# A three-part transformer program on one core: new SBUF addresses for its stages, with the weights and inner activations of the long stage shifted by 32, 64 and 192 bytes

## The chip, the cores and the metric

One core of one Trainium2 chip. The metric is the device time of one execution in microseconds (us). The profile is one profiled execution of the same program.

## The reference, cut to what matters

Two transformer blocks follow each other on 1024 tokens of width 1024, in fp32. In outline (the three stages that the text names are marked):

```
z = rms_norm(x) @ w_in                      # "pp": projections of block 1, latent queries/keys/values
o_g = gated_linear_attention(...) * silu(g_r)
o_m = latent_attention(...)
h = x + concat(o_g, o_m) @ w_out            # "rm", the long stage, begins here
h = h + square(relu(rms_norm(h) @ w_mlp_up)) @ w_mlp_down
h = h + (p @ w_ple_proj) * sigmoid(rms_norm(h) @ w_ple_gate + b)
q, k, v, z = modulated(rms_norm(h)), modulated(ctx) @ da_w_in      # "rm" ends here
o = softmax differences over 1280 keys, 8 heads                     # "da"
out = rms_norm(h + gate * ((norm(o) * silu(z)) @ da_w_out))         # "hp"
```

## The kernel before, in words

The program is a chain of blocks, each ended by a barrier of all engines: pp (`project_and_prepare`), gla, ma, rm (`residual_to_differential`), da (`differential_attention`), hp (`head_norm_project`). Every fp32 product is made of three fp32r matmuls on a high and a low part: stationary hi with moving hi, stationary hi with moving lo, stationary lo with moving hi (`product`, line 242; lines 874 to 876 in pp). Each matmul comes with its own weight load of 128 columns (PEld); the load for the next matmul runs while the present one streams. Names in the profile read out<-moving,stationary.

**The long stage, rm.** Weight chunks of 128x512 go through a ring `rm_stage` of four (SP loads them, ACT makes `rm_w_hi`, POOL `rm_w_lo`). In order: the output projection (16 tiles of 24 matmuls, x stationary, w moving); eight groups of the MLP, each 8 "up" tiles (24 matmuls each, w stationary, x moving, 512 columns) and then 16 "down" tiles (12 matmuls each, the inner activations `rm_h_hi`/`rm_h_lo` stationary, w moving); the gate (16 tiles of 24, x stationary) and `p @ w_ple_proj` (16 tiles of 6); the projections of block 2: z, q and k (48 tiles of 24, w stationary, x moving), their context tiles (8 tiles of 24 with 256 columns, `ctx_hi`/`ctx_lo` moving), and v (20 tiles of 24, w moving, x stationary in 16 of them, ctx in 4).

**Addresses.** Tensors are given addresses in the order of the `sb(...)` calls, upward and without gaps; what opens in an inner context is placed over what a closed one held. Bytes in a partition, from the declared shapes:

| tensor | before | modulo 512 |
|---|---|---|
| x halves (`xa`, `xb`, hi and lo), all stages | from 50336 | 160 |
| `rm_stage` | 115872 | 160 |
| `rm_w_hi`, `rm_w_lo` | 124064, 156832 | 160, 160 |
| `rm_h_hi`, `rm_h_lo` | 196032, 212416 | 448, 448 |
| `ctx_hi`, `ctx_lo` | 196032, 204224 | 448, 448 |
| `rm_pT`, `rm_proj` | from 196032 | 448 |
| `pp_w_hi`, `pp_w_lo` | 124064, 140448 | 160, 160 |
| da: q, k, v, aT, prob | from 50848 | 160 |
| `hp_w`, x in hp | from 124576, 50848 | 160 |

In every matmul operand a 128-column slice or a row of k is a multiple of 512 bytes, so the remainder above is that of each access. "Distance" below is the stationary operand's address minus the moving one's, modulo 512.

**The end of pp.** For the last token tile (t = 7) PE turns four groups of queries and keys (`turn`, line 916, four transposes each into the one bank `turn_bank`), ACT copies each to `pp_qk_hi` (`high`, line 614), DVE subtracts into `pp_qk_lo` (`low`, line 784), and SP stores both (lines 449, 451). Each `turn` waits until the `low` before it has read the bank. The groups of output columns of pp are taken in the order of `first_col`: two of features, two of `gv`, two of `gr` (the gate, with Silu instead of Copy in `take`, line 573).

Of the kernel before, what the change touches and what calls it, by code (L numbers as in the profile page):

```python
# [12 lines left out]
P = 128  # L13
# [33 lines left out]
class Chip:  # L47
# [7 lines left out]

    def sb(self, name, shape, dt=F32, ctx=None):
        return (ctx or self.ctx).enter_context(self.nc.sbuf_tensor(name, shape, dt))

# [19 lines left out]
    def place_differential(self):  # L78

        keys = S + CTX
        with ExitStack() as ctx:
            sb = lambda name, shape, dt=F32: self.sb("da_" + name, shape, dt, ctx)
            sb("sums_place", [P, DH * TT, 2])
            prob, aT_lo = sb("prob", [P, 4, 2, keys]), sb("aT_lo", [P, 2, keys // P, 2 * P], F32R)
            low_score, inv, ratio = sb("low_score", [P, DH * TT, 2]), sb("inv", [P, DH * TT]), sb("ratio", [P, DH * TT])
            lam_in, lam_prod = sb("lam_in", [P, 2, 2, DD]), sb("lam_prod", [P, 2, DD])
            sb("space_a", [P, 256])
            q0 = sb("q0", [P, 2, S], F32R)  # L90
            k_hi0, v_hi0 = sb("k_hi0", [P, 2, keys], F32R), sb("v_hi0", [P, keys // P, P], F32R)
            sb("space_b", [P, 256])
            q1, v_hi1 = sb("q1", [P, 2, S], F32R), sb("v_hi1", [P, keys // P, P], F32R)
            sb("space_c", [P, 768])
            k_lo0, v_lo0 = sb("k_lo0", [P, 2, keys], F32R), sb("v_lo0", [P, keys // P, P], F32R)
            k_hi1, k_lo1 = sb("k_hi1", [P, 2, keys], F32R), sb("k_lo1", [P, 2, keys], F32R)
            v_lo1 = sb("v_lo1", [P, keys // P, P], F32R)
            aT_hi = sb("aT_hi", [P, 2, keys // P, 2 * P], F32R)
            o_sb = sb("o_sb", [P, 2, NCOL])
        self.da = dict(prob=prob, aT_lo=aT_lo, aT_hi=aT_hi, low_score=low_score, inv=inv, ratio=ratio, lam_in=lam_in,  # L100
                       lam_prod=lam_prod, o_sb=o_sb, q=(q0, q1), k_hi=(k_hi0, k_hi1), k_lo=(k_lo0, k_lo1),
                       v_hi=(v_hi0, v_hi1), v_lo=(v_lo0, v_lo1))
# [39 lines left out]
def constants(nc, chip, a):  # L142

    c = chip
    c.H = c.sb("residual", [P, TT, D])
    c.sums = c.sb("sums", [P, TT])
# [102 lines left out]
def project_and_prepare(nc, chip, a, d):  # L249
# [14 lines left out]
    c_q = g_r + GH * GDV  # L264
    first_col = [None, 0, GW, NCOL, NCOL + GW, g_r, g_r + GW]
    FEATURE = (1, 2)
# [16 lines left out]
    with ExitStack() as ctx:  # L283
# [8 lines left out]
        junk = free[:, at:at + 1280]  # L292
        stage = sb("stage", [P, SLOTS, NCOL])
        piece_stage = stage[:].rearrange("p a (b n) -> p (a b) n", b=2)
        w_hi, w_lo = sb("w_hi", [P, KT, 2 * GW], F32R), sb("w_lo", [P, KT, 2 * GW], F32R)
        with ExitStack() as early:
# [25 lines left out]
        ssh, msh, rsh = sb("ssh", [P, 2, 2, MH]), sb("msh", [P, 2, 2, MH]), sb("rsh", [P, 2, 2, MH])  # L322
        v_hi, v_lo = sb("v_hi", [P, MH, MV], F32R), sb("v_lo", [P, MH, MV], F32R)
        up_bank = c.banks("pp_up", ctx, 4)
        c_bank, turn_bank = c.banks("pp_turn", ctx, 2)
# [27 lines left out]

        tok_of = lambda t: slice(t * P, (t + 1) * P)

        def x_bank(t, b):
# [26 lines left out]
        def result(n):  # L383

            g, o = outs[n]
            bank = p_bank[n % 2]
            if g in FEATURE:
                f, h = divmod(o, HALVES)
                return bank[:], ring[:, n % RING, :], d["gqk"][2 * (g - 1) + f, :, h * NCOL:(h + 1) * NCOL]
            name = "gv" if g < 5 else "gr"  # L390
            cols = slice((g - 3) % 2 * GW, (g - 3) % 2 * GW + GW)
            return bank[:, 0:GW], ring[:, n % RING, 0:GW], d[name][o][:, cols]
# [148 lines left out]
        def _(act):  # L541
# [16 lines left out]
            def take(n):  # L558
# [12 lines left out]
                if n - first_out[1] >= RING:  # L571
                    act.wait_ge(stored[n % RING], 16 * stores_at(n - RING))
                nc.scalar.activation(held, bank, ACT.Silu if g >= 5 else ACT.Copy,
                                     scale=GDK ** -0.5 if g == 1 else 1.0).then_inc(copied, 1)
# [34 lines left out]
            def high(t, m):  # L609
                q, g = divmod(m, 2)  # L610
                act.wait_ge(turned, 4 * t + m + 1)
                if t:
                    act.wait_ge(q_out, 64 * t)
                nc.scalar.activation(qk_hi[:, q, 4 * g:4 * g + 4, :],
                                     turn_bank[0:MQK].rearrange("p (h n) -> p h n", h=4), ACT.Copy).then_inc(hi_ready, 1)

# [61 lines left out]
        def _(dve):  # L678
# [102 lines left out]
            def low(t, m):  # L781
                q, g = divmod(m, 2)
                dve.wait_ge(hi_ready, 4 * t + m + 1)
                nc.vector.tensor_tensor(qk_lo[:, q, 4 * g:4 * g + 4, :],
                                        turn_bank[0:MQK].rearrange("p (h n) -> p h n", h=4),
                                        qk_hi[:, q, 4 * g:4 * g + 4, :].bitcast(F32), ALU.subtract).then_inc(lo_ready, 1)
# [65 lines left out]
        def _(pe):  # L852
# [58 lines left out]
            def turn(t, m):  # L911
                q, g = divmod(m, 2)
                pe.wait_ge(roped, 4 * t + 2 * (q + 1))
                pe.wait_ge(*((lo_ready, 4 * t + m) if 4 * t + m else (x_lo_ready, 2 * TT)))
                for h in range(4):
                    last = nc.tensor.transpose(turn_bank[0:MQK, h * P:(h + 1) * P], nrm[:, t % 2, q, 4 * g + h, :],
                                               c.ident[:])
# [885 lines left out]
def residual_to_differential(nc, chip, a, d):  # L1803
# [58 lines left out]
    with ExitStack() as ctx:  # L1862
        sb = lambda n, s, dt=F32: c.sb("rm_" + n, s, dt, ctx=ctx)
        sem = lambda n: c.sem("rm_" + n, ctx)
        stage = sb("stage", [P, SLOTS, NCOL])
        w_hi, w_lo = sb("w_hi", [P, 2, KT, NCOL], F32R), sb("w_lo", [P, 2, KT, NCOL], F32R)
        act_r = sb("act_r", [P, 2, NCOL])
        scaled = act_r[:].rearrange("p a n -> p (a n)")
        mean, rstd = sb("mean", [P, 3, TILES]), sb("rstd", [P, 3, TILES])
        ctx_sums = sb("ctx_sums", [P, CT])  # L1870
        full2 = sb("full", [P, NCOL])
        with ExitStack() as early:
            h_hi, h_lo = (c.sb(f"rm_h_{x}", [P, FT, S], F32R, ctx=early) for x in ("hi", "lo"))
        with ExitStack() as middle:
# [7 lines left out]
        table = dsb("table", [P, 2, NCOL])  # L1882
        x, swapped = dsb("x", [P, 2, NCOL]), dsb("swapped", [P, 2, NCOL])
        out_lo = act_r
        full = (bias[:, 0:NCOL], full2[:])
# [705 lines left out]
def differential_attention(nc, chip, a, d):  # L2591
# [17 lines left out]
    with ExitStack() as ctx:  # L2609
        sb = lambda n, s, dt=F32: c.sb("da_" + n, s, dt, ctx=ctx)  # L2610
        sem = lambda n: c.sem("da_" + n, ctx)
        sb("place", [P, 42880])
        q, k_hi, k_lo, v_hi, v_lo = (c.da[x] for x in ("q", "k_hi", "k_lo", "v_hi", "v_lo"))
# [224 lines left out]
def head_norm_project(nc, chip, a, d, out):  # L2838
# [13 lines left out]
    with ExitStack() as ctx:  # L2852
        sb = lambda n, s, dt=F32: c.sb("hp_" + n, s, dt, ctx=ctx)
        sem = lambda n: c.sem("hp_" + n, ctx)
        w = Weights(c, "hp", ctx, groups)
        o, z, sq = sb("o", [P, DH, NCOL]), sb("z", [P, ZS, NCOL]), sb("sq", [P, 2, NCOL])
# [6 lines left out]
        final_gain = z[:, 0:2].rearrange("p a n -> p (a n)")  # L2863
        mean, rstd = sb("mean", [P, TT]), sb("rstd", [P, TT])
        sum_bank = c.banks("hp_sum", ctx, 2)
        wide_bank = c.banks("hp_wide", ctx, 2)
# [365 lines left out]
```

## Time and profile before

| | |
|---|---|
| median of 3 runs | 2427.17 us (2419.51 to 2428.51) |
| the profiled execution | 2428.71 us, its span 2426.9 us |
| TensorE (PE) busy | 2274.8 us, 94% of the span |
| PE weight loads (PEld) | 1889.2 us, 78% |
| DVE, ACT, POOL | 46%, 40%, 35% |
| mean granted TensorE clock | 0.968 of full speed |

The page gives for each engine the busy time and its share of the span, and the granted clock in 40 slices. The end of a matmul is modelled, so a busy PE says that matmuls follow each other, not how fast; how fast comes from the starts in the timeline.

### The profile page before, as it was taken

How to read it: one execution, taken by the hardware profiler on the slowest of the kernel's cores; microseconds unless marked ns; L12 is line 12 of the kernel's file. 1: busy time of each engine (PE TensorE's matmuls, PEld its weight loads, DVE VectorE, ACT ScalarE, POOL GpSimd, SP SyncE). 2: the span in 40 equal slices, each digit the busy share in tenths (PEclk: the TensorE clock that was granted, in tenths of full speed). 3: DMA queues.
4: the chain of work that ended last, by engine and by line, in shares of the span. 5: the costliest groups of instructions: out<-in, count | busy, mean ns of one | idle time of the engine just before them, and what ended most of it. 6: DMA issues, size and time to landing. Idle time of an engine off the chain costs nothing. (4 is left out here: it accounts for less than half of the span.)

```text
span 2426.9 us, 31960 instructions
## 1 busy us (share of the span) xinstructions
PE 2274.8 (94%) x12292; PEld 1889.2 (78%) x12292; DVE 1126.7 (46%) x1992; ACT 976.5 (40%) x1993; POOL 861.4 (35%) x755
## 2 busy tenths in 40 slices
PE   6999487979999999999999999999999899999798
PEld 6799346967888888888887887888888688888566
DVE  4555486861522222222223535044421788888435
ACT  5434344861523113112113426233221677677422
POOL 5433153543323123123123216332210577777331
PEclk9999688999999999999999999999999899999999
DMA  5455745522111112012012112366656335533231
GB/s 149 104 159 132 226 166 166 135 67 74 46 54 57 33 50 70 25 50 66 29 46 65 57 35 66 113 177 204 188 149 179 100 92 128 142 96 96 100 126 78
DMA packets 202281, 248.48 MB, mean 102 GB/s; under 512 B 63592, under 2 KB 123384, under 8 KB 202128
## 3 DMA queue, kind: packets, MB, share of 16 engines
q1 hardware_dynamic: 196368, 240.14, 34.5%
q10 hardware_dynamic: 5760, 6.29, 0.8%
q8 instruction: 97, 1.59, 0.3%
q14 instruction: 56, 0.46, 0.1%
HBM read 172.88 MB, written 65.10 MB: 98 GB/s over the span
## 5 line engine op out<-in xcount | busy, mean ns | idle before, releaser
L2088 POOL TENSOR_TENSOR rm_w_lo<-rm_stage,rm_w_hi 128x512 fp32r<-128x512 f32 x192 | 246.8, 1298 | 653.8 <-ACT rm_w_hi L2158 653.2
L2158 ACT ACTIVATE rm_w_hi<-rm_stage 128x512 fp32r<-128x512 f32 x192 | 118.2, 628 | 287.8 <-PE rm_down L242 234.4
L2795 DVE TENSOR_REDUCE da_low_score<-da_scores 128x1 f32<-128x1280 f32 x128 | 190.3, 1488 | 31.2 <-PE da_scores L2675 31.1
L242 PE MATMUL rm_down<-rm_w_hi,rm_h_hi 128*128 128x512 f32 x512 | 203.7, 398 | 0.0
L242 PE MATMUL rm_down<-rm_w_lo,rm_h_hi 128*128 128x512 f32 x512 | 203.0, 396 | 0.0
L242 PE MATMUL rm_down<-rm_w_hi,rm_h_lo 128*128 128x512 f32 x512 | 202.9, 396 | 0.0
L2346 DVE TENSOR_TENSOR residual<-residual,rm_down 128x512 f32<-128x512 f32 x128 | 87.5, 687 | 225.8 <-PE rm_down L242 225.1
L2778 POOL TENSOR_TENSOR da_prob<-da_prob 128x1280 f32<-128x1280 f32 x64 | 188.2, 2941 | 5.3
L2736 ACT ACTIVATE da_prob<-da_scores,da_low_score 128x1280 f32<-128x1280 f32 x128 | 170.7, 1334 | 7.3 <-DVE da_low_score L2795 7.3
L2675 PE MATMUL da_scores<-da_k_hi,da_q 128*128 128x512 f32 (+1 forms) x384 | 151.7, 395 | 20.3 <-ACT da_prob L2736 9.2
L2337 DVE TENSOR_TENSOR rm_act_r<-rm_act_r 128x512 f32<-128x512 f32 x64 | 45.5, 711 | 222.2 <-ACT rm_act_r L2201 222.2
L2776 POOL TENSOR_SCALAR da_prob<-da_prob,da_ratio 128x1280 f32<-128x1280 f32 x64 | 86.0, 1343 | 173.4 <-DVE da_ratio L2803 173.2
L2675 PE MATMUL da_scores<-da_k_lo,da_q 128*128 128x512 f32 (+1 forms) x384 | 133.7, 364 | 0.0
L2745 ACT ACTIVATE da_aT_hi<-da_turn 128x512 fp32r<-128x512 f32 (+1 forms) x192 | 94.8, 532 | 62.9 <-PE da_turn L2689 62.7
L2810 DVE TENSOR_TENSOR da_aT_lo<-da_turn,da_aT_hi 128x512 fp32r<-128x512 f32 (+1 forms) x192 | 109.1, 596 | 22.1 <-ACT da_aT_hi L2745 20.3
L2201 ACT ACTIVATE rm_act_r<-rm_up 128x512 f32<-128x512 f32 x64 | 38.5, 601 | 194.0 <-PE rm_up L242 193.9
L242 PEld LDWEIGHTS rm_down<-rm_w_hi,rm_h_lo 128*128 128x128 f32 x512 | 96.5, 189 | 23.5
L242 PEld LDWEIGHTS rm_down<-rm_w_lo,rm_h_hi 128*128 128x128 f32 x512 | 96.6, 189 | 23.1
L242 PEld LDWEIGHTS rm_down<-rm_w_hi,rm_h_hi 128*128 128x128 f32 x512 | 96.6, 189 | 23.0
L242 PE MATMUL rm_up<-xa_hi,rm_w_hi 128*128 128x512 f32 x288 | 113.1, 393 | 0.7 <-POOL xb_lo L2116 0.7
L242 PE MATMUL rm_up<-xa_lo,rm_w_hi 128*128 128x512 f32 x288 | 112.7, 391 | 0.0
L242 PE MATMUL rm_up<-xb_hi,rm_w_hi 128*128 128x512 f32 x288 | 112.1, 389 | 0.5 <-POOL rm_w_lo L2088 0.5
(395 smaller groups left out, 6216.4 us busy)
## 6 DMA issues: line engine op xcount, KB each, us to landing
rm_stage<-in_w_mlp_up SPq DMA_DIRECT2D x64, 256.0 KB, 2.8
rm_stage<-in_w_mlp_down SPq DMA_DIRECT2D x64, 256.0 KB, 2.9
rm_stage<-in_da_w_in SPq DMA_DIRECT2D x64, 256.0 KB, 3.3
gla_ada_w<-in_ada_w SPq DMA_DIRECT2D x12, 1024.0 KB, 6.9
da_k_hi<-dk_hi SPq DMA_DIRECT2D x32, 320.0 KB, 7.5
da_k_lo<-dk_lo SPq DMA_DIRECT2D x32, 320.0 KB, 9.1
dp_swapped<-dp_x SPq DMA_DIRECT2D x128, 64.0 KB, 2.0
da_q<-dq SPq DMA_DIRECT2D x32, 256.0 KB, 6.1
```

Of the source, the lines that this page charges most:

```text
L242: last = nc.tensor.matmul(out, x, y, start=(n == 0), stop=(n == total - 1))
L2088: nc.gpsimd.tensor_tensor(lo, stage[:, n % SLOTS], hi.bitcast(F32), ALU.subtract).then_inc(w_lo_ready, 1)
L2158: nc.scalar.activation(hi, stage[:, n % SLOTS], ACT.Copy).then_inc(w_hi_ready, 1)
L2337: nc.vector.tensor_tensor(act_r[:, n % 2], act_r[:, n % 2], act_r[:, n % 2], ALU.mult)\
L2346: nc.vector.tensor_tensor(c.H[:, t, cols_of(half)], c.H[:, t, cols_of(half)], down_bank[n % 5][:], ALU.add).then_inc(down_added, 1)
L2675: last = nc.tensor.matmul(scores[z][:, at:end], q[s][:, z, qt * P:(qt + 1) * P], k[s][:, z, at:end], start=(i == 0), stop=(i == 1))
L2736: nc.scalar.activation(prob[:, n % BUF, z], scores[z][:, 0:K], ACT.Exp, scale=-1.0, bias=low_score[:, n, z:z + 1], accum_out=sums[:, n, z: ...
L2745: nc.scalar.activation(aT_hi[:, n // 2 % 2, j:e, (n % 2) * P:(n % 2 + 1) * P], turn_bank(i)[:, 0:(e - j) * P].rearrange("p (j q) -> p j q" ...
L2776: nc.gpsimd.tensor_scalar(p1, p1, ratio[:, n:n + 1], 1.0, ALU.mult, ALU.mult).then_inc(rest_scaled, 1)
L2778: nc.gpsimd.tensor_tensor(p0, p0, p1, ALU.add).then_inc(prob_ready, 1)
L2795: nc.vector.tensor_reduce(out=low_score[:, n, z:z + 1], in_=scores[z][:, 0:K], op=ALU.min, axis=AX.X).then_inc(low_score_ready, 1)
L2810: nc.vector.tensor_tensor(aT_lo[:, n // 2 % 2, j:e, q], turn_bank(i)[:, 0:(e - j) * P].rearrange("p (j q) -> p j q", q=P), aT_hi[:, n // 2 ...
```

## The change

The residual `c.H` is placed at the right end of the memory, the scratch for descriptors at its left end shrinks from 16384 to 1024 bytes, and the buffers of each stage are placed anew. In rm, `rm_h_hi` and the ctx tensors come first, 32 bytes lie between `rm_h_hi` and `rm_h_lo`, and 64 and 128 further bytes ahead of `rm_w_hi` and `rm_w_lo`. In da, `k_lo` and `v_lo` of even heads lie 192 bytes off the rest; in hp a spacer keeps the weights at x's remainder. In pp the ring and the weights move behind the other buffers. The same sums give:

| tensor | after | modulo 512 |
|---|---|---|
| x halves, all stages but hp | from 2208 | 160 |
| `rm_h_hi`, `ctx_hi`, `ctx_lo` | 67744, 67744, 75936 | 160 |
| `rm_h_lo` | 84160 | 192 |
| `rm_w_hi` | 114912 | 224 |
| `rm_w_lo` | 147808 | 352 |
| `rm_stage` | 106656 | 160 |
| `rm_pT`, `rm_proj` | from 67744 | 160 |
| `pp_w_hi`, `pp_w_lo` | 148192, 164576 | 224 |
| da: `k_lo0`, `v_lo0` | 147808, 158048 | 352 |
| da: all else; hp: x and w | | 160 |

Two edits of pp are no addresses: the gate's columns (`gr`, Silu) are now groups 3 and 4 and those of `gv` groups 5 and 6, and the last token tile's turns use two banks in alternation (`head_bank`), so that each waits for the `low` before the last one.

```diff
@@ -53,8 +53,8 @@
-    def sb(self, name, shape, dt=F32, ctx=None):
-        return (ctx or self.ctx).enter_context(self.nc.sbuf_tensor(name, shape, dt))
+    def sb(self, name, shape, dt=F32, ctx=None, side=None):
+        return (ctx or self.ctx).enter_context(self.nc.sbuf_tensor(name, shape, dt, side=side))
@@ -87,16 +87,18 @@
             sb("space_a", [P, 256])
+            aT_hi = sb("aT_hi", [P, 2, keys // P, 2 * P], F32R)
+            o_sb = sb("o_sb", [P, 2, NCOL])
+            sb("space_d", [P, 3584])
             q0 = sb("q0", [P, 2, S], F32R)
...
             q1, v_hi1 = sb("q1", [P, 2, S], F32R), sb("v_hi1", [P, keys // P, P], F32R)
-            sb("space_c", [P, 768])
+            sb("space_c", [P, 816])
             k_lo0, v_lo0 = sb("k_lo0", [P, 2, keys], F32R), sb("v_lo0", [P, keys // P, P], F32R)
+            sb("space_e", [P, 208])
             k_hi1, k_lo1 = sb("k_hi1", [P, 2, keys], F32R), sb("k_lo1", [P, 2, keys], F32R)
             v_lo1 = sb("v_lo1", [P, keys // P, P], F32R)
-            aT_hi = sb("aT_hi", [P, 2, keys // P, 2 * P], F32R)
-            o_sb = sb("o_sb", [P, 2, NCOL])
         self.da = dict(prob=prob, aT_lo=aT_lo, aT_hi=aT_hi, low_score=low_score, inv=inv, ratio=ratio, lam_in=lam_in,
@@ -142,7 +144,7 @@
     c = chip
-    c.H = c.sb("residual", [P, TT, D])
+    c.H = c.sb("residual", [P, TT, D], side="right")
     c.sums = c.sb("sums", [P, TT])
@@ -262,7 +264,8 @@
     c_q = g_r + GH * GDV
-    first_col = [None, 0, GW, NCOL, NCOL + GW, g_r, g_r + GW]
+    first_col = [None, 0, GW, g_r, g_r + GW, NCOL, NCOL + GW]
+    GATE = (3, 4)
     FEATURE = (1, 2)
@@ -290,9 +293,6 @@
         junk = free[:, at:at + 1280]
-        stage = sb("stage", [P, SLOTS, NCOL])
-        piece_stage = stage[:].rearrange("p a (b n) -> p (a b) n", b=2)
-        w_hi, w_lo = sb("w_hi", [P, KT, 2 * GW], F32R), sb("w_lo", [P, KT, 2 * GW], F32R)
         with ExitStack() as early:
@@ -321,6 +321,9 @@
         v_hi, v_lo = sb("v_hi", [P, MH, MV], F32R), sb("v_lo", [P, MH, MV], F32R)
+        stage = sb("stage", [P, SLOTS, NCOL])
+        piece_stage = stage[:].rearrange("p a (b n) -> p (a b) n", b=2)
+        w_hi, w_lo = sb("w_hi", [P, KT, 2 * GW], F32R), sb("w_lo", [P, KT, 2 * GW], F32R)
         up_bank = c.banks("pp_up", ctx, 4)
@@ -353,6 +356,10 @@
+        def head_bank(t, m):
+
+            return up_bank[0] if t == TT - 1 and m % 2 else turn_bank
+
         def x_bank(t, b):
@@ -612,7 +619,8 @@
                 nc.scalar.activation(qk_hi[:, q, 4 * g:4 * g + 4, :],
-                                     turn_bank[0:MQK].rearrange("p (h n) -> p h n", h=4), ACT.Copy).then_inc(hi_ready, 1)
+                                     head_bank(t, m)[0:MQK].rearrange("p (h n) -> p h n", h=4), ACT.Copy)\
+                    .then_inc(hi_ready, 1)
@@ -911,9 +919,10 @@
                 pe.wait_ge(roped, 4 * t + 2 * (q + 1))
-                pe.wait_ge(*((lo_ready, 4 * t + m) if 4 * t + m else (x_lo_ready, 2 * TT)))
+                read = 4 * t + m - (1 if t == TT - 1 and m else 0)
+                pe.wait_ge(*((lo_ready, read) if read else (x_lo_ready, 2 * TT)))
                 for h in range(4):
-                    last = nc.tensor.transpose(turn_bank[0:MQK, h * P:(h + 1) * P], nrm[:, t % 2, q, 4 * g + h, :],
+                    last = nc.tensor.transpose(head_bank(t, m)[0:MQK, h * P:(h + 1) * P], nrm[:, t % 2, q, 4 * g + h, :],
                                                c.ident[:])
@@ -1862,15 +1871,10 @@
-        stage = sb("stage", [P, SLOTS, NCOL])
-        w_hi, w_lo = sb("w_hi", [P, 2, KT, NCOL], F32R), sb("w_lo", [P, 2, KT, NCOL], F32R)
-        act_r = sb("act_r", [P, 2, NCOL])
-        scaled = act_r[:].rearrange("p a n -> p (a n)")
-        mean, rstd = sb("mean", [P, 3, TILES]), sb("rstd", [P, 3, TILES])
-        ctx_sums = sb("ctx_sums", [P, CT])
-        full2 = sb("full", [P, NCOL])
...
-            h_hi, h_lo = (c.sb(f"rm_h_{x}", [P, FT, S], F32R, ctx=early) for x in ("hi", "lo"))
+            h_hi = c.sb("rm_h_hi", [P, FT, S], F32R, ctx=early)
+            c.sb("rm_space_h", [P, 8], ctx=early)
+            h_lo = c.sb("rm_h_lo", [P, FT, S], F32R, ctx=early)
@@ -1881,6 +1885,17 @@
+        sb("space", [P, 1536])
+        stage = sb("stage", [P, SLOTS, NCOL])
+        sb("space_hi", [P, 16])
+        w_hi = sb("w_hi", [P, 2, KT, NCOL], F32R)
+        sb("space_lo", [P, 32])
+        w_lo = sb("w_lo", [P, 2, KT, NCOL], F32R)
+        act_r = sb("act_r", [P, 2, NCOL])
+        scaled = act_r[:].rearrange("p a n -> p (a n)")
+        mean, rstd = sb("mean", [P, 3, TILES]), sb("rstd", [P, 3, TILES])
+        ctx_sums = sb("ctx_sums", [P, CT])
+        full2 = sb("full", [P, NCOL])
@@ -2609,7 +2624,7 @@
         sem = lambda n: c.sem("da_" + n, ctx)
-        sb("place", [P, 42880])
+        sb("place", [P, 46720])
         q, k_hi, k_lo, v_hi, v_lo = (c.da[x] for x in ("q", "k_hi", "k_lo", "v_hi", "v_lo"))
@@ -2852,7 +2867,6 @@
         sem = lambda n: c.sem("hp_" + n, ctx)
-        w = Weights(c, "hp", ctx, groups)
         o, z, sq = sb("o", [P, DH, NCOL]), sb("z", [P, ZS, NCOL]), sb("sq", [P, 2, NCOL])
@@ -2862,6 +2876,8 @@
         mean, rstd = sb("mean", [P, TT]), sb("rstd", [P, TT])
+        sb("space_w", [P, 96])
+        w = Weights(c, "hp", ctx, groups)
         sum_bank = c.banks("hp_sum", ctx, 2)
@@ -3218,7 +3234,7 @@
-    nc = bacc.Bacc("TRN2", target_bir_lowering=False, num_devices=1)
+    nc = bacc.Bacc("TRN2", target_bir_lowering=False, num_devices=1, dynamic_dma_scratch_size=1024)
     arrays, args = {}, {}
```

## Rows read from the trace of the kernel before

**Rows 1.** The page: span, TensorE's busy time, the granted clock in 40 slices.
```profile
span 2426.9 us, 31960 instructions
...
PE 2274.8 (94%) x12292; PEld 1889.2 (78%) x12292; DVE 1126.7 (46%) x1992; ACT 976.5 (40%) x1993; POOL 861.4 (35%) x755
...
PEclk9999688999999999999999999999999899999999
```

**Rows 2.** Busy time by stretch (busy us and instructions per engine, clock, DMA share, GB/s).
```profile
150.00:250.00 100.00, 100.00 (x799) 98.96 (x798) 51.98 (x126) 40.38 (x101) 29.29 (x31) 1.00 0.55 144
...
640.00:1313.00 673.00, 672.48 (x2935) 549.37 (x2934) 175.83 (x268) 154.84 (x275) 159.91 (x127) 1.00 0.16 49
...
1500.00:1880.00 380.00, 379.71 (x1779) 317.88 (x1778) 116.31 (x190) 105.88 (x225) 87.75 (x100) 1.00 0.56 166
1880.00:2280.00 400.00, 366.93 (x2383) 325.49 (x2381) 324.11 (x485) 272.90 (x483) 274.19 (x128) 0.97 0.39 101
```

**Rows 3.** Timeline of PE (start us, us): first matmuls of three runs of 192.
```profile
688.74 0.39 PE L242 MATMUL rm_down<-rm_w_hi,rm_h_hi 128*128 128x512 f32 x1
...
733.53 0.39 PE L242 MATMUL rm_up<-xa_hi,rm_w_hi 128*128 128x512 f32 x1
...
777.06 0.39 PE L242 MATMUL rm_down<-rm_w_hi,rm_h_hi 128*128 128x512 f32 x1
```

**Rows 4.** Groups of PE's instructions by shape (busy us, mean ns of one).
```profile
L242 PE MATMUL rm_down<-rm_w_lo,rm_h_hi 128*128 128x512 f32 x512 | 203.0, 396 | 0.0
...
L242 PE MATMUL rm_up<-xb_hi,rm_w_lo 128*128 128x512 f32 x288 | 112.1, 389 | 0.0
...
L242 PE MATMUL rm_down<-rm_w_lo,xb_hi 128*128 128x512 f32 x180 | 70.0, 389 | 0.0
...
L242 PE MATMUL rm_down<-rm_w_lo,ctx_hi 128*128 128x512 f32 x32 | 12.7, 395 | 0.0
```

**Rows 5.** Timeline of PE: 48 matmuls of v's context tiles, first, and what follows.
```profile
1817.31 0.39 PE L242 MATMUL rm_down<-rm_w_hi,ctx_hi 128*128 128x512 f32 x1
...
1828.50 0.39 PE L242 MATMUL rm_up<-rm_w_hi,xa_hi 128*128 128x512 f32 x1
```

**Rows 6.** Timeline of PE: 48 and 96 matmuls of 256 columns, first and next.
```profile
243.04 0.36 PE L874 MATMUL pp_ps<-pp_w_hi,x_hi 128*128 128x256 f32 x1
...
248.87 0.49 PE L916 MATMUL pp_turn<-ident,residual 128*96 128x128 f32 x3
...
1707.81 0.28 PE L242 MATMUL rm_down<-ctx_hi,rm_w_hi 128*128 128x256 f32 x1
...
1719.01 0.39 PE L242 MATMUL rm_down<-xa_hi,rm_w_hi 128*128 128x512 f32 x1
```

**Rows 7.** Timeline at the end of pp, [idle before <- who ended it].
```profile
259.48 0.59 ACT L614 ACTIVATE pp_qk_hi<-pp_turn 96x512 fp32r<-96x512 f32 x1 [0.53 <-DMA mqk_lo<-pp_qk_lo]
...
260.10 0.69 DVE L784 TENSOR_TENSOR pp_qk_lo<-pp_turn,pp_qk_hi 96x512 fp32r<-96x512 f32 x1 [1.33 <-ACT pp_qk_hi L614]
260.94 1.06 PE L916 MATMUL pp_turn<-ident,residual 128*96 128x128 f32 x4 [1.97 <-DVE pp_qk_lo L784]
262.03 0.59 ACT L614 ACTIVATE pp_qk_hi<-pp_turn 96x512 fp32r<-96x512 f32 x1 [1.96 <-PE pp_turn L916]
...
267.77 0.69 DVE L784 TENSOR_TENSOR pp_qk_lo<-pp_turn,pp_qk_hi 96x512 fp32r<-96x512 f32 x1 [1.87 <-ACT pp_qk_hi L614]
...
268.83 0.54 SPq L451 DMA_DIRECT2D mqk_lo<-pp_qk_lo  x1
...
273.75 1.28 ACT L1122 ACT_TABLE_LOAD   x1 [6.01 <-PEq L283]
```

**Rows 8.** Timeline of ACT: the table load ahead of pp's first Silu.
```profile
202.72 1.28 ACT L573 ACT_TABLE_LOAD   x1
```

**Rows 9.** Waits of PE in da, 1920 to 2260 us (total us, times, longest).
```profile
PE da_scores L2675 <- DMA da_k_lo<-dk_lo: 8.7, 5, 2.1
```

More of the change, by code:

```diff
@@ L389, in result @@
                 return bank[:], ring[:, n % RING, :], d["gqk"][2 * (g - 1) + f, :, h * NCOL:(h + 1) * NCOL]
-            name = "gv" if g < 5 else "gr"
+            name = "gr" if g in GATE else "gv"
             cols = slice((g - 3) % 2 * GW, (g - 3) % 2 * GW + GW)
@@ L572, in take @@
                     act.wait_ge(stored[n % RING], 16 * stores_at(n - RING))
-                nc.scalar.activation(held, bank, ACT.Silu if g >= 5 else ACT.Copy,
+                nc.scalar.activation(held, bank, ACT.Silu if g in GATE else ACT.Copy,
                                      scale=GDK ** -0.5 if g == 1 else 1.0).then_inc(copied, 1)
@@ L784, in low @@
                 nc.vector.tensor_tensor(qk_lo[:, q, 4 * g:4 * g + 4, :],
-                                        turn_bank[0:MQK].rearrange("p (h n) -> p h n", h=4),
+                                        head_bank(t, m)[0:MQK].rearrange("p (h n) -> p h n", h=4),
                                         qk_hi[:, q, 4 * g:4 * g + 4, :].bitcast(F32), ALU.subtract).then_inc(lo_ready, 1)
```

## The prediction

> **What bounds the kernel now.** I read the page first: TensorE's 2274.8 us of 2426.9 us, and a granted clock of 9 or 10 tenths in nearly all slices [rows 1], its upper level of 2.4 GHz. The windows by stretch then show where PE has no gap: the second half of pp (100.00 of 100 us), the MLP (672.48 of 673), the projections of block 2 (379.71 of 380); in da it has some gaps (366.93 of 400) [rows 2]. In these stretches nothing counts but how fast one matmul follows another, and a busy share can't show that, since the ends are modelled. So I went to the starts in the timeline. One "down" group of the MLP, 192 matmuls of 512 columns, runs from 688.74 to 733.53: 44.79 us, 233.3 ns each. The "up" group behind it, also 192 of 512 columns, runs from 733.53 to 777.06: 43.53 us, 226.7 ns each [rows 3]. The same work, without a wait in either, differs by 6.6 ns a matmul, 2.9%.
>
> What differs? By the table of addresses, in "up" both operands have remainder 160 (distance 0), in "down" the inner activations have 448 and the weights 160 (distance 288). It could be a property of "down" tiles instead, which are only 12 matmuls long and whose operands DVE and ACT have just written. Against that stand the context tiles of v: 24 matmuls long, ctx stationary at 448, weights moving at 160, distance 288 again. 48 of them take 1817.31 to 1828.50, 11.19 us, 233.1 ns each [rows 5]. The groups by shape say the same: a mean of 396 ns with `rm_h` and 395 with ctx, but 389 with x stationary under the same moving weights, and 389 in "up" [rows 4]. So I read the pair of addresses as the cause. With 256 columns there is a third distance: context columns moving at 448 under weights at 160, distance 224, take 1707.81 to 1719.01 for 96, 116.7 ns each; pp's, at distance 0, take 243.04 to 248.87 for 48, 121.5 ns each [rows 6]. So distance 0 is not shown to be the best: 288 is worse by 6.6 ns at 512 columns, 224 is better by 4.8 ns at 256.
>
> The Trainium skill (SBUF — State Buffer, "Who interferes with whom") says that PE has two independent read ports, one for the moving operand and one for the weight load, and that PE never waits on anyone. By that rule addresses can't matter and the long stage would not move at all; the rows above speak against it, and it stands below as a rival.
>
> **The change, part by part.** The sum goes against the profiled execution's 2428.7 us; the median of the runs is 1.5 us less, and I take that off at the end.
>
> 1. *Distances that go.* At 288 today are 8 groups x 192 = 1536 "down" matmuls and 4 tiles x 24 = 96 of v: 1632. After the change "down" has distances of -64 (w_hi moving, h_hi stationary or loading) and -160 (w_lo moving while h_lo is loaded); v's context tiles have -64 and -192. No row has any of these four. If they are as good as 0, each matmul gains 6.6 ns [rows 3]: 1632 x 6.57 = 10.7 us, all on the path, since PE has no gap there [rows 2] and its feeders are at half load or less. The bounds: 0 (as bad as 288) to 6.57 + 4.8 = 11.4 ns (as much better than 0 as distance 224 is [rows 6]): 18.6 us. I take 10.7.
>
> 2. *Distances that come.* "Up" and the z, q, k tiles, 1536 + 48 x 24 = 2688 matmuls, go from 0 to +64 (two of three) and +192 (one of three). Output projection, gate and v's x tiles, 384 + 384 + 384 = 1152, go from 0 to -64 and -192. Together 3840. The bounds are +6.57 ns (as 288): +25.2 us, and -4.8 ns: -18.4 us. Between them I take 0, the row of distance 0 at 512 columns itself, because the two measured other distances lie on either side of it. This is the term that decides the sign, and no row settles it.
>
> 3. *The weights of pp* go 64 bytes off x: 192 matmuls of 512 columns, 192 of 432, 768 of 256. Price 0 in between -4.8 x 1152 = -5.5 us and +6.57 x 1152 = +7.6 us.
>
> 4. *da.* `k_lo` and `v_lo` of even heads go 192 off: 32 query tiles x 2 x 3 score matmuls and 32 x 5 value matmuls, 352. At 6.57 ns that is 2.3 us either way; 0 taken. PE's waits there for `da_k_lo` to land, 8.7 us [rows 9], stay: loads and their order are the same. `rm_pT` and `rm_proj` keep a common remainder (96 matmuls), hp too. Both 0.
>
> 5. *The end of pp.* Today turn, copy and subtraction go round in 2.55 us (ACT at 259.48 and 262.03), four times, and the last subtraction ends at 267.77 + 0.69 = 268.46 [rows 7]. With two banks the second turn is over before the first copy begins. First subtraction 260.10 to 260.79 and then the second to 261.5; the third turn still starts at 260.94 and lasts 1.06, its copy starts at 262.03; the fourth turn follows at 262.0 and ends at 263.1, copy to 263.7, last subtraction to about 264.4. So 268.46 - 264.4 = 4.0 us earlier. Behind it the store issued at 268.83 and its landing and barrier until 273.75 [rows 7] are late as before: 4.9 us, unchanged and not hidden, so the 4.0 us go through in full. The copies of the group still wait for the stores of the tile before (0.53 us at 259.48), which is in the sum. Bounds: 0 if the turns wait for something I don't see, 5.1 if the third turn too comes at once.
>
> 6. *Order of gate and values.* The Silu's table load of 1.28 us at 202.72 [rows 8] comes two groups earlier; PE has no idle time there before or after, since from 150 to 250 it is busy throughout [rows 2]. The same number of stores goes out. 0. What covers it is the second bank of results; without that cover it would cost 1.28 us.
>
> 7. *The residual at the right end, less scratch, spacers.* No instruction is added. 0.
>
> Sum: -10.7 - 4.0 = -14.7, from 2428.7 to 2414.0; as a median 2412.5.
>
> **The rivals.** (B) *The new distances are better than 0.* For it: the 4.8 ns at distance 224 [rows 6]. Against it: that was at 256 columns, against a stretch broken by transposes. Two thirds of that gain on all 5472 matmuls, 3.2 ns, adds 17.5 us: 2395. All of it: 2386.
>
> (C) *Any distance but 0 costs what 288 costs.* Then "down" stays at 233.3 ns and 3840 matmuls join it: +25.2 - 4.0 = +21.2, 2448.4. For it: at 512 columns both rows that exist follow this rule. Against it: 224. The point from which it decides: a loss of 0.7 ns on each of the 3840 eats the 4.0 us of the end of pp once "down" gains nothing. Its place is the "up" group, which would take 44.8 us where it takes 43.5.
>
> (D) *Addresses have no part in it*, or the tensors don't come to lie where my sums put them in relation to each other. The long stage keeps its time and the end of pp alone is left: 2423.2. The rule of the skill named above gives this. Against it: the two kinds of tile at 448 and the three at 160 [rows 3 to 5].
>
> A further ground stands apart: the Trainium skill (TensorE: Matmul & The Clock Gate, "Back-to-back issue gap") gives N/2.4 + 2.5 ns for warm matmuls, 215.8 ns at 512 columns. If the 226.7 of [rows 3] were conflict throughout and the new distances removed it, an estimate from that page would be (226.7 - 215.8) x 5472 = 60 us less on top of case A; but that gap is for matmuls without a weight load between them, and no row comes near it.
>
> **How the numbers follow.** My forecast (A): 0.37, 2412.5. B: 0.20, 2386 to 2400. C: 0.23, half of the pairs to all of them, 2432 to 2449. D: 0.15, 2423. What is left, 0.05, is a gain beyond B. The range of 2388 to 2449 leaves out the end of B, what lies beyond it and the overrun of C by pp and da, some 0.15. The likeliest case alone, with the bounds of terms 3 to 5, is 2405 to 2420. A measurement here can tell about 0.5%, 12 us: faster is below 2415, slower above 2439. Faster: two thirds of A, B and what lies beyond, 0.49. Slower: the larger part of C, 0.21. Within 0.5%: 0.30, the rest of A, D and the small losses.
>
> **What would show it.** In the timeline of the changed kernel: a "down" group of 192 in 43.5 us (A), 44.8 (C); an "up" group in 43.5 (A, D), 44.8 (C), under 43.1 (B); in pp the last `pp_qk_lo` some 4 us earlier against the last result tile, and the next stage's table load about 269.7. In the groups by shape the mean of `rm_down<-rm_w_lo,rm_h_hi` falls from 396 to 389. The prediction is wrong if matmuls with +64 or +192 between their addresses take other than 226 to 228 ns.

## The result and the profile after

The changed kernel takes 2435.44 us (median of 6 runs, 2433.47 to 2439.36), the kernel before in the same session 2425.07 us (6 runs, 2419.51 to 2428.51). The ratio is 1.0046, with a 95% interval of 1.0031 to 1.0061: slower by about half a per cent, where I had forecast 0.6% faster. The profiled execution took 2433.83 us. The page of the changed kernel, the rows that answer to [rows 1]:

```profile
span 2432.0 us, 31960 instructions
...
PE 2277.4 (94%) x12292; PEld 1873.2 (77%) x12292; DVE 1126.0 (46%) x1992; ACT 974.8 (40%) x1993; POOL 866.2 (36%) x755
...
PEclk9999688999999999999999999999999999999999
```

The page tells almost nothing: the same number of instructions, TensorE's share the same, the granted clock's digits the same but for one slice around 1900 us (8 before, 9 now; 9 stands for the upper level, 2.4 GHz, nearly throughout). The windows answer to [rows 2]; the number to read is the count of PE's instructions (x...) behind its busy time:

```profile
150.00:250.00 100.00, 100.00 (x814) 99.03 (x814) 52.49 (x128) 38.84 (x99) 29.17 (x30) 1.00 0.54 142
...
640.00:1313.00 673.00, 672.54 (x2898) 542.86 (x2897) 172.32 (x258) 151.00 (x266) 158.03 (x123) 1.00 0.16 48
```

In the MLP's 673 us PE is as busy as before (672.54 against 672.48) and gets through 2898 instructions instead of 2935: 1.3% fewer without an idle moment more. In pp (150 to 250) it gets through 814 instead of 799, 1.9% more. In both windows PE has no gap, so it is the pace of the matmuls that changed: slower in the long stage, quicker in pp.

The timeline of PE of the changed kernel (start us, us, form) gives the pace of each kind of tile. These rows answer to [rows 3], [rows 5] and the second pair of [rows 6]:

```profile
538.05 0.79 PE L244 MATMUL rm_down<-rm_w_hi,xa_hi 128*128 128x512 f32 x1 [9.68 <-POOL rm_w_lo L2103]
...
683.74 0.40 PE L244 MATMUL rm_down<-rm_w_hi,rm_h_hi 128*128 128x512 f32 x1
...
728.52 0.39 PE L244 MATMUL rm_up<-xa_hi,rm_w_hi 128*128 128x512 f32 x1
...
773.03 0.40 PE L244 MATMUL rm_down<-rm_w_hi,rm_h_hi 128*128 128x512 f32 x1
...
1715.35 0.28 PE L244 MATMUL rm_down<-ctx_hi,rm_w_hi 128*128 128x256 f32 x1
...
1726.28 0.39 PE L244 MATMUL rm_down<-xa_hi,rm_w_hi 128*128 128x512 f32 x1
...
1781.72 0.39 PE L244 MATMUL rm_down<-rm_w_hi,xa_hi 128*128 128x512 f32 x1
...
1825.95 0.39 PE L244 MATMUL rm_down<-rm_w_hi,ctx_hi 128*128 128x512 f32 x1
...
1837.01 0.39 PE L244 MATMUL rm_up<-rm_w_hi,xa_hi 128*128 128x512 f32 x1
...
1894.65 0.47 PE L2690 MATMUL da_scores<-da_k_hi,da_q 128*128 128x512 f32 x1 [2.19 <-PEq L1871]
...
2292.07 1.01 PE L3015 MATMUL hp_sum<-hp_sq,hp_band 128*4 128x512 f32 x1 [7.67 <-ACT hp_sq L2964]
```

- The "down" group of 192 lasts from 683.74 to 728.52: 44.78 us, where it took 44.79. It gained nothing.
- The "up" group lasts from 728.52 to 773.03: 44.51 us, 231.8 ns a matmul, where it took 43.53 us, 226.7 ns.
- The x tiles of v (192 matmuls, weights moving) take 44.23 us, 230.4 ns; v's context tiles (48) 11.06 us, 230.4 ns, where they took 233.1.
- The context matmuls of 256 columns (96) take 10.93 us, 113.9 ns, where they took 116.7.

The same landmarks in the kernel before (first `rm_down`, first score, first product of hp):

```profile
545.95 0.80 PE L242 MATMUL rm_down<-rm_w_hi,xa_hi 128*128 128x512 f32 x1 [10.36 <-POOL rm_w_lo L2088]
...
1885.58 0.70 PE L2675 MATMUL da_scores<-da_k_hi,da_q 128*128 128x512 f32 x1 [2.19 <-PEq L1862]
...
2286.51 1.01 PE L2999 MATMUL hp_sum<-hp_sq,hp_band 128*4 128x512 f32 x1 [7.60 <-ACT hp_sq L2948]
```

Between first `rm_down` and first score lie 1356.60 us against 1339.63: +17.0. All that comes before is 7.9 us shorter (538.05 against 545.95), da 3.5 us shorter (397.42 against 400.93), the end 0.5. 17.0 - 7.9 - 3.5 - 0.5 = 5.1, the difference of the two spans.

The medians differ by more, 10.4 us. Two parts of the 5.1 are likely to belong to this pair of executions rather than to the change. In the first 100 us the mean granted clock is 0.93 before and 0.97 now, and pp's first matmul of 512 columns starts at 85.04 and at 82.36: 2.7 us of the 7.9 (`common`, with the same pp but for the last turns, has 0.95 and 84.19). And da's 3.5 us go with a granted clock of 0.99 instead of 0.97 between 1880 and 2280 us. Without these two the difference would be 11.3 us, near that of the medians.

### The profile page after: what moved, and what is told of

It is laid out like the page before. It is cut to its first block and busy times, and to the rows that moved or that the text cites. A ratio compares the mean times of both kernels' runs of the same rounds, so it can differ in the third digit from the quotient of the medians.

```text
span 2432.0 us, 31960 instructions
## 1 busy us (share of the span) xinstructions
PE 2277.4 (94%) x12292; PEld 1873.2 (77%) x12292; DVE 1126.0 (46%) x1992; ACT 974.8 (40%) x1993; POOL 866.2 (36%) x755
## 5 line engine op out<-in xcount | busy, mean ns | idle before, releaser
L244 PE MATMUL rm_up<-xa_hi,rm_w_lo 128*128 128x512 f32 x288 | 114.2, 397 | 0.0
L244 PE MATMUL rm_up<-xb_hi,rm_w_lo 128*128 128x512 f32 x288 | 114.2, 397 | 0.0
```

What stands on the lines that cost most here:

```text
L244: last = nc.tensor.matmul(out, x, y, start=(n == 0), stop=(n == total - 1))
```

## Experiments

My theory from here on (T1): the *distance* between the stationary and the moving operand sets the interval, and the multiple of 512 is a good one. Against it: T2 (the absolute remainder counts), T3 ("down" is slow because of what it is), D (addresses have no part).

**All distances back to 0: `common`.** The changed kernel without its offsets; all else stays (the second turn bank, the order of the gate, pp's weights at +64).

```diff
-            sb("space_c", [P, 816])
+            sb("space_c", [P, 768])
-            sb("space_e", [P, 208])
+            sb("space_e", [P, 256])
-            c.sb("rm_space_h", [P, 8], ctx=early)
-        sb("space_hi", [P, 16])
-        sb("space_lo", [P, 32])
```

> All products of the long stage at distance 0 (down and v's context tiles too), pp and the rest as in the change. T1 (the distance between stationary and moving operand sets the interval, and 0 is the one that locks at 226.7 ns): the up group stays or returns to 43.5 us and the down group of 192 falls from 44.8 to 43.5 us; the long stage takes about 1335 us (1345.9 before, 1362.3 with the change), the kernel about 2408. T3 (down tiles are slow because of what they are, not where they lie): down stays at 44.8 and the kernel is at about 2418. D (addresses have no part; the change lost for another reason): up stays at 44.5, no gain over the change, about 2434.

2408.25 us (6 runs, 2406.33 to 2414.62), ratio to the kernel before 0.9939 (0.9923 to 0.9955): faster than both kernels. PE's timeline:

```profile
539.73 0.80 PE L244 MATMUL rm_down<-rm_w_hi,xa_hi 128*128 128x512 f32 x1 [9.60 <-POOL rm_w_lo L2100]
...
682.89 0.39 PE L244 MATMUL rm_down<-rm_w_hi,rm_h_hi 128*128 128x512 f32 x1
...
726.41 0.39 PE L244 MATMUL rm_up<-xa_hi,rm_w_hi 128*128 128x512 f32 x1
...
769.93 0.39 PE L244 MATMUL rm_down<-rm_w_hi,rm_h_hi 128*128 128x512 f32 x1
...
1691.85 0.28 PE L244 MATMUL rm_down<-ctx_hi,rm_w_hi 128*128 128x256 f32 x1
...
1703.36 0.40 PE L244 MATMUL rm_down<-xa_hi,rm_w_hi 128*128 128x512 f32 x1
...
1869.60 0.47 PE L2687 MATMUL da_scores<-da_k_hi,da_q 128*128 128x512 f32 x1 [2.19 <-PEq L1871]
...
2266.62 1.01 PE L3012 MATMUL hp_sum<-hp_sq,hp_band 128*4 128x512 f32 x1 [7.64 <-ACT hp_sq L2961]
```

"Down" and "up" both take 43.52 us, and the long stage 1329.87 us (first `rm_down` to first score), 9.8 less than before and 26.7 less than with the change. T3 and D fall. The context matmuls of 256 columns go the other way: 96 in 11.51 us, 119.9 ns, slower than before (116.7) and with the change (113.9).

**The one distance of before mended by itself: `before_h_160`.** A spacer in the kernel before moves the inner activations and the context from remainder 448 to 160.

```diff
         full2 = sb("full", [P, NCOL])
+        sb("space", [P, 56])
         with ExitStack() as early:
```

> The kernel before with the inner activations and the context moved 224 bytes, from remainder 448 to 160; nothing else changed. T1: term 1 of my prediction alone, -10.7 us (down group 43.5 us, v's context tiles 226.7 ns), kernel at about 2414; the context matmuls of 256 columns go from 116.7 to about 119.7 ns (+0.4 us at most). T3 or D: no difference, down group 44.8 us.

2413.89 us (7 runs, 2410.26 to 2415.18), ratio 0.9959 (0.9944 to 0.9973). PE's timeline:

```profile
687.54 0.39 PE L242 MATMUL rm_down<-rm_w_hi,rm_h_hi 128*128 128x512 f32 x1
...
731.06 0.39 PE L242 MATMUL rm_up<-xa_hi,rm_w_hi 128*128 128x512 f32 x1
...
774.58 0.39 PE L242 MATMUL rm_down<-rm_w_hi,rm_h_hi 128*128 128x512 f32 x1
```

Again 43.52 us for both. One spacer of 224 bytes and not one instruction more or less is worth 9.9 us of the median. This is my term 1 alone, and it was right for distance 0.

**Everything moved by 64 bytes: `shift_64`.** `common` with one more spacer of 64 bytes ahead of all stages.

```diff
     c.minus_half = c.sb("minus_half", [P, 64])
+    c.sb("space_all", [P, 16])
```

> As common, but every tensor of the left side lies 64 bytes further right (remainder 224 instead of 160), all distances unchanged at 0. T1: the same intervals as in common, up and down groups 43.5 us. T2 (the absolute remainder of an operand matters, not the distance): the groups move, most likely to 44.5 us as the operands at 224 had in the change.

```profile
687.03 0.39 PE L245 MATMUL rm_down<-rm_w_hi,rm_h_hi 128*128 128x512 f32 x1
...
730.55 0.39 PE L245 MATMUL rm_up<-xa_hi,rm_w_hi 128*128 128x512 f32 x1
```

The "down" group takes 43.52 us, the "up" group behind it, which ends at 774.07, the same (one run, 2414.67 us): T2 falls for this shift. Weights at remainder 224 beside x at 160 were slow in the change; here 224 beside 224 is fast. It is the distance that counts.

**Five other distances: `w_plus_32`, `w_plus_128`, `w_plus_256`, `w_minus_64`, `w_minus_160`.** `common` with a spacer ahead of both weight tensors of the long stage; the spacers of da follow. "Up", z, q and k then lie at +d, "down", output, gate and v at -d. The diff for +128 (the others: 8, 64, 112 and 88 floats):

```diff
+        sb("space_hi", [P, 32])
         w_hi = sb("w_hi", [P, 2, KT, NCOL], F32R)
-            sb("space_c", [P, 768])
+            sb("space_c", [P, 800])
-            sb("space_e", [P, 256])
+            sb("space_e", [P, 224])
```

> As common, but both weight tensors of the long stage lie 128 bytes off (up, z, q, k at +128; down, output, gate and v at -128), one distance alone in a group. T1 with 'no distance but 0 locks': up and down groups between 44.2 and 44.8 us. T1b (it is the mixing of two distances within one tile, +64 and +192, that disturbs the pace in the change, not the distance itself): both groups at 43.5 us. D: 43.5 for up, 44.8 for down.

> common with both weight tensors of the long stage 32 bytes off (up at +32, down at -32), the smallest step. T1: not at 226.7 ns any more; with the 233 ns of +128 the long stage takes about 1361 us and the kernel about 2442. Rival T1c (only a distance of 64 or more counts): the groups of 192 stay at 43.5 us and the kernel at 2410.

> common with both weight tensors 256 bytes off, where plus and minus are the same. T1: up and down groups equal to each other, 44.2 to 44.8 us; kernel 2430 to 2442. If a distance better than 0 exists (rival B), the middle between the multiples of 512 is the likeliest place: groups below 43.5 us, the kernel below 2400.

> common with both weight tensors 64 bytes below (up at -64, down at +64), one distance in each group. By the means of the change and of pp: up 232.8 ns (44.7 us), down 233.3 ns (44.8 us), kernel about 2442. If pp's 229.6 ns at -64 (the run with pp at +64) is right instead: up 44.1 us, kernel about 2435.

> common with both weight tensors 160 bytes below (up at -160, down at +160). In the change the pairs at -160 took 230.9 ns mixed with others. T1: up and down groups between 44.2 and 44.8 us, none below 43.5, kernel 2430 to 2442. Rival B would have one of the signs below 43.5 us.

PE's timeline of `w_plus_128`, then of `w_plus_32`, `w_plus_256`, `w_minus_64` and `w_minus_160`:

```profile
685.70 0.40 PE L244 MATMUL rm_down<-rm_w_hi,rm_h_hi 128*128 128x512 f32 x1
...
730.49 0.40 PE L244 MATMUL rm_up<-xa_hi,rm_w_hi 128*128 128x512 f32 x1
...
775.29 0.40 PE L244 MATMUL rm_down<-rm_w_hi,rm_h_hi 128*128 128x512 f32 x1
```

```profile
687.20 0.40 PE L244 MATMUL rm_down<-rm_w_hi,rm_h_hi 128*128 128x512 f32 x1
...
732.00 0.40 PE L244 MATMUL rm_up<-xa_hi,rm_w_hi 128*128 128x512 f32 x1
...
776.79 0.39 PE L244 MATMUL rm_down<-rm_w_hi,rm_h_hi 128*128 128x512 f32 x1
```

```profile
682.65 0.39 PE L244 MATMUL rm_down<-rm_w_hi,rm_h_hi 128*128 128x512 f32 x1
...
726.17 0.39 PE L244 MATMUL rm_up<-xa_hi,rm_w_hi 128*128 128x512 f32 x1
...
769.69 0.39 PE L244 MATMUL rm_down<-rm_w_hi,rm_h_hi 128*128 128x512 f32 x1
```

```profile
730.08 0.40 PE L244 MATMUL rm_up<-xa_hi,rm_w_hi 128*128 128x512 f32 x1
...
774.88 0.39 PE L244 MATMUL rm_down<-rm_w_hi,rm_h_hi 128*128 128x512 f32 x1
...
819.68 0.40 PE L244 MATMUL rm_up<-xa_hi,rm_w_hi 128*128 128x512 f32 x1
...
863.64 0.39 PE L244 MATMUL rm_down<-rm_w_hi,rm_h_hi 128*128 128x512 f32 x1
```

```profile
687.13 0.40 PE L244 MATMUL rm_down<-rm_w_hi,rm_h_hi 128*128 128x512 f32 x1
...
731.94 0.39 PE L244 MATMUL rm_up<-xa_hi,rm_w_hi 128*128 128x512 f32 x1
...
776.91 0.40 PE L244 MATMUL rm_down<-rm_w_hi,rm_h_hi 128*128 128x512 f32 x1
```

Together, each group being a difference of two starts:

| kernel | up at, us of 192 | down at, us of 192 | one run, us |
|---|---|---|---|
| `common` | 0, 43.52 | 0, 43.52 | 2408.25 (median) |
| `w_plus_32` | +32, 44.79 | -32, 44.80 | 2445.61 |
| `w_minus_64` | -64, 44.80 or 43.96 | +64, 44.80 | 2438.15 |
| `w_plus_128` | +128, 44.80 | -128, 44.79 | 2444.27 |
| `w_minus_160` | -160, 44.97 | +160, 44.81 | 2442.71 |
| `w_plus_256` | +256, 43.52 | -256, 43.52 | 2407.11 |

(0.01 us is the rounding of a start.) +128 alone costs as much as the whole of 288 did, so the mixing of two distances isn't what hurts (T1b falls); 32 bytes already cost it (T1c falls). At 256 I missed: I had expected 44.2 to 44.8 us, and it is exactly as good as 0 (at -160 the "up" group, with 44.97, lies a little above what I expected). The simplest reading is that the distance counts **modulo 256**: with 512 columns, 0 is the fast one, and 32, 64, 96, 128 and their negatives are slow (96 stands for the two of 160). 288, the distance of before, is 32. That the period is 256 rests on this one run; its context matmuls of 256 columns, 96 in 11.51 us, are those of distance 0 too.

**pp's weights: `pp_at_0` and `pp_plus_64`.** `common` with a spacer ahead of pp's weights (112 or 96 floats), which puts them on x's remainder or 64 bytes below it.

```diff
+        sb("space_w", [P, 96])
         stage = sb("stage", [P, SLOTS, NCOL])
         piece_stage = stage[:].rearrange("p a (b n) -> p (a b) n", b=2)
```

> common, with pp's weights back at distance 0, the whole kernel then at 0. T1 by the rows of before: 768 matmuls of 256 columns go back from 117 to 119.7 ns (+2.1 us) and 192 of 512 columns from 233 to 226.7 ns (-1.2 us), those of 432 columns lose some 2 ns more (+0.4): kernel 1 to 2 us slower than common. If pp's weights are what made pp some 4 us shorter: 4 us slower.

> common, with pp's weights 64 bytes below x instead of 64 above it (remainder 96), so that its 768 matmuls of 256 columns (x stationary, weights moving) have a distance of +64, at which the context matmuls of 256 columns took 113.9 ns in the change, where pp's took about 117 ns at -64; its 192 matmuls of 512 columns get -64 (232.8 ns there, 233.3 at +64). T1: 768 x 3.1 = 2.4 us less than common, 2406 us. If the sign has no part in it: 117 ns stay and the time is that of common.

`pp_at_0` 2415.03 us (4 runs, 2405.59 to 2417.0), ratio 0.9956 (0.9938 to 0.9973); `pp_plus_64` 2407.54 us (6 runs, 2401.78 to 2411.27), ratio 0.9929 (0.9916 to 0.9943). The windows of `pp_at_0`, then of `pp_plus_64`:

```profile
150.00:250.00 100.00, 100.00 (x800) 98.96 (x799) 52.55 (x127) 38.44 (x99) 29.27 (x31) 1.00 0.55 143
```

```profile
150.00:250.00 100.00, 100.00 (x823) 99.07 (x822) 52.65 (x127) 39.47 (x101) 29.77 (x31) 1.00 0.55 145
```

In the same 100 us PE does 800 instructions at distance 0, 814 at -64 (the changed kernel and `common`) and 823 at +64. With 256 columns the order is the other way round from 512: of these three, 0 is slowest. What it is worth comes from the starts of pp's matmuls in the timeline (us); its 192 matmuls of 512 columns come first, then the 768 of 256 columns, at the opposite distance:

| kernel | distance at 256 columns | first of 512 columns | first of 256 | last of 256 | 512 part | 256 part |
|---|---|---|---|---|---|---|
| before | 0 | 85.04 | 143.55 | 258.25 | 58.51 | 114.70 |
| `pp_at_0` | 0 | 84.33 | 142.88 | 257.48 | 58.55 | 114.60 |
| changed | -64 | 82.36 | 141.50 | 254.02 | 59.14 | 112.52 |
| `common` | -64 | 84.19 | 143.19 | 255.92 | 59.00 | 112.73 |
| `pp_plus_64` | +64 | 84.54 | 143.19 | 254.59 | 58.65 | 111.40 |

Against `pp_at_0`, `common` gains 1.9 us in the part of 256 columns and loses 0.5 in that of 512, 1.4 us in all; `pp_plus_64` gains 3.1. The traces show the order. The times alone would not: the intervals of `common`, `pp_at_0` and `pp_plus_64` overlap, `pp_plus_64` and `common` are the two best versions with several runs, and I can't tell them apart by their times.

**The end of pp: `one_bank`.** `common` with all head turns in the one bank.

```diff
-            return up_bank[0] if t == TT - 1 and m % 2 else turn_bank
+            return turn_bank
-                read = 4 * t + m - (1 if t == TT - 1 and m else 0)
+                read = 4 * t + m
```

> common, with all head turns of the last tile in the one turn bank again. Expected: the four last rounds of turn, copy and subtraction go back from 4.0 to 9.0 us, the last subtraction ends 5 us later against the first copy, and the next stage's table load comes 3.8 to 5 us later. If the second bank brought nothing: the same end of pp as in common.

The timeline at the end of pp, of the changed kernel and then of `one_bank`:

```profile
255.44 0.59 ACT L621 ACTIVATE pp_qk_hi<-pp_turn 96x512 fp32r<-96x512 f32 x1 [0.71 <-DMA mqk_lo<-pp_qk_lo]
...
256.90 0.61 PE L925 MATMUL pp_turn<-ident,residual 128*96 128x128 f32 x4 [1.72 <-DVE pp_qk_lo L792]
...
257.73 0.54 SPq L458 DMA_DIRECT2D mqk_lo<-pp_qk_lo  x1
...
258.78 0.68 DVE L792 TENSOR_TENSOR pp_qk_lo<-pp_up,pp_qk_hi 96x512 fp32r<-96x512 f32 x1
...
259.84 1.49 SPq L458 DMA_DIRECT2D mqk_lo<-pp_qk_lo  x1
265.90 1.28 ACT L1131 ACT_TABLE_LOAD   x1 [7.16 <-PEq L286]
```

```profile
256.98 0.59 ACT L621 ACTIVATE pp_qk_hi<-pp_turn 96x512 fp32r<-96x512 f32 x1 [0.76 <-DMA mqk_lo<-pp_qk_lo]
...
264.82 0.69 DVE L792 TENSOR_TENSOR pp_qk_lo<-pp_turn,pp_qk_hi 96x512 fp32r<-96x512 f32 x1 [1.87 <-ACT pp_qk_hi L621]
...
265.89 0.54 SPq L458 DMA_DIRECT2D mqk_lo<-pp_qk_lo  x1
270.80 1.28 ACT L1131 ACT_TABLE_LOAD   x1 [6.01 <-PEq L286]
```

From the first copy to the end of the last subtraction: 4.02 us with two banks (255.44 to 259.46), 8.53 with one (256.98 to 265.51), 8.98 before. (The 0.45 between the last two is one turn of four transposes: the first one behind the first copy takes 0.61 us in `one_bank`, at 258.44, and 1.06 before, at 260.94 [rows 7]. There the granted clock is 0.50, its lower level, from 260.9 to 268.) From that end to the table load: 6.44 us with two banks, 5.29 with one and 5.29 before. The second bank saves 4.5 to 5.0 us and 1.15 us come back behind it: the issue of the last store takes 1.49 us instead of 0.54 where it comes 2.1 us behind the one before (257.73, 259.84), and 0.54 where it comes 5.1 us behind (260.77, 265.89). The other kernels with two banks show it too, again 2.1 us behind: 1.47 us in `common`, 1.61 in `shift_64`, 1.46 in `pp_plus_64`. That the short distance in time is the reason is likely, but no run parts it from what else differs there. What goes through is 3.8 us against the kernel before, 3.4 against `one_bank` (13.82 against 10.46). `one_bank` took 2416.47 us in its one run.

**The order of gate and values: `gate_late`.** `common` with `first_col` and `GATE = (5, 6)` as in the kernel before.

> common, with the values ahead of the gate again. Expected: pp's last head copies at the same time within 0.5 us (my term 6 was 0). Rival: the gate behind the values lengthens the end of pp, since the last copies of results wait for their stores; then the first of the four last copies comes 1 to 2 us later.

One run, 2411.3 us. The window from 150 to 250 has 816 instructions of PE against 814, and the first of the last copies comes at 258.17, where it comes at 257.37 in `common`, 257.32 in `shift_64`, 256.98 in `one_bank` and 255.44 in the changed kernel, which all have the same pp but for the last turns. A difference of 0.8 us is less than their spread of 1.9. From the first to the last start of pp's 768 matmuls of 256 columns it takes 112.53 us, `common` 112.73: no cost of the order shows there.

## Why the prediction was wrong

1. **Term 1 (the distances that go, -10.7): failed.** The step that failed is "if they are as good as 0". Going from 288 to 0 is worth what I said (`before_h_160`: 44.79 to 43.52 us a group, 9.3 us of the stage, from 543.98 to 1874.32 where it was 1339.63 us long; it would be some 0.6 more, but the 192 context matmuls of 256 columns slow down by 3.2 ns each). But the change doesn't put "down" at 0; it puts it at -64 and -160, and both are as slow as 288. Gain: 0 in "down" (44.78 us a group), 2.7 ns x 96 = 0.3 us in v's context tiles.

2. **Term 2 (the distances that come, 0): failed, and it decided the sign**, as the prediction said it would. Measured: "up" 8 groups x 0.98 = 7.8 us; z, q and k at 232.0 ns (taken from those 600 of their matmuls that follow each other without a break, 139.19 us from 1576.16 to 1715.35), 1152 x 5.2 = 6.0; v's x tiles +3.5 ns, the output tiles +2.9 (24 matmuls in 5.61 instead of 5.54 us), the gate +3.2 (5.54 instead of 5.46), 384 of each, 3.7. Less 0.3 for v's context and 192 x 2.8 = 0.5 for the context matmuls: 16.7 us, and the stage shows 17.0. The prediction named its own sign of failure, +64 or +192 taking other than 226 to 228 ns; they take 231.8. I had taken 0 because "the two measured other distances lie on either side of it". That bracket joined a row of 512 columns with a row of 256 [rows 3, 6], and `common` and the five distances show that the two widths rank the distances differently. It also overstated the row of 256: the 121.5 ns of pp's 48 matmuls hold a break between two tiles, and in `common` distance 0 takes 119.9 ns, so distance 224 is better by 3.2 ns and not 4.8. With the rows of 512 columns alone the only guide was "what isn't 0 costs 6.6 ns", which was rival C.

3. **Term 3 (pp's weights, 0; bounds -5.5 to +7.6):** by the table above, 2.2 us were gained in the part of 256 columns and 0.6 lost in that of 512: -1.6, inside the bounds. Until the first of the last copies the changed kernel is 4.0 us ahead; most of the rest is the 2.7 us by which it is ahead at the start of the 512 part, where the granted clock of the first 100 us was the higher one.

4. **Term 4 (da, 0):** da was 3.5 us shorter in this trace. But `common`, whose da operands have the distances of before, has nearly the same, 397.02 us (1869.60 to 2266.62). So it isn't the offset. The granted clock between 1880 and 2280 us goes the same way, 0.97 before, 0.99 with the change and 0.98 in `common`; how much of the 3.5 us it makes, no run shows.

5. **Term 5 (the end of pp, -4.0): right**, 3.8 us, but by two errors that cancel, so the hit is luck. The rounds got 5.0 us shorter, not 4.0: the third turn starts 1.46 us behind the first copy in both kernels (260.94 and 256.90), as I had said, but it and the fourth take 0.61 us where I had taken the 1.06 of [rows 7]. They now run while the clock is still at its upper level (granted clock 1.00 between 254.0 and 258.4). And the store behind them is not "late as before" but 1.15 us slower.

6. **Terms 6 and 7 (0):** nothing speaks against them.

With what was measured the sum is 16.7 - 1.6 - 3.8 = +11.3 us, where the medians differ by +10.4.

**The rivals.** C held, in a milder form: 5.1 of the 6.57 ns for "up", 3.5 for v, nothing gained in "down". Its "half of the pairs", given as 2432 us, should by its own prices read 2427.2 + 12.6 - 4.0 = 2435.8, and that this meets the 2435.4 measured is luck: some two thirds of the 25.2 us were lost, and pp gave a part back. Its sign was 44.8 us in "up", and the group took 44.51. Its turning point was reckoned wrong: 4.0 us on 3840 matmuls are 1.0 ns and not 0.7. It was passed more than fourfold (17.5 us on 3840 are 4.6 ns). B fell at 512 columns: none of the distances tried is below 43.52 us a group. D fell with `common` and `before_h_160`: two programs with the same instructions differ by 9.9 us through the place of a few tensors. The Trainium skill (SBUF — State Buffer, "Who interferes with whom") says that PE never waits on anyone; in this kernel PE's pace does depend on where its two operands lie, so the measurement decides against it here. No kernel here came below 226.7 ns at 512 columns in a steady run. The estimate of 215.8 ns by the Trainium skill (TensorE: Matmul & The Clock Gate, "Back-to-back issue gap") was not approached, as the prediction expected.

**What stays open.** Why the pace depends on the distance: the runs show how it goes with the distance, not the mechanism. Why one distance has two paces: at -64 the "up" groups of `w_minus_64` take 44.80 and 43.96 us by turns through the whole MLP, and later tiles with x moving 228.9 ns (120 matmuls from 1599.49 to 1626.96); at 128 the MLP takes 233.3 ns and the later tiles 232.4. The mixtures of the change are partly explained: if +192 counts as -64, the mean of two matmuls at 233.3 ns and one at 228.9 is 231.8, as measured in "up", and of one and two 230.4, as in v. That is a second ground for the period of 256. But "down", at -64 and -160, stays at 233.3 ns and does not follow this mean. Distances under 32 bytes weren't tried.

## What to carry to other kernels

When a stage is bound by TensorE without gaps, compare groups of equal matmuls by the starts in the timeline, and if two groups differ by a few per cent, look at the addresses: with 512 fp32r columns and a new stationary operand for every matmul, put both on the same remainder modulo 256 (here 2.9% of the pace, for one spacer). Don't carry the choice to other widths, since at 256 columns this distance was among the slowest here. And a bracket made of two rows that differ in a second thing, here the width, bounds nothing.

## What was not expected of the hardware

- With 512 columns the pace is the same at a distance of 256 bytes as at 0, 43.52 us for 192 matmuls, and 44.8 to 45.0 at 32, 128 and 160 between them. 226.7 ns is 544 cycles of 2.4 GHz, 233.3 ns is 560.
- At 256 columns these two are among the slowest, 119.9 ns (`common`, `w_plus_256`; 120.1 at +128, `w_plus_128` from 1720.98 to 1732.51), against 116.7 before (distance 224) and 113.9 with the change (+64 and +192).
- Shifting both operands by 64 bytes left the groups of 192 at 43.52 us.
- Of 5 us taken out of a tail 1.15 came back in the stores behind it, which then stood closer together (an issue of 1.49 us instead of 0.54).
